# Where squares, low products and norm sums stand at the seams of a two-block network on one core

## What is computed

```python
h = h + 0.5 * rmsnorm_2(swiglu(rmsnorm_2(h, norm_g[0]), ffn1_gu, ffn1_down), norm_g[1])
z = rmsnorm_2(h, norm_g[2]) @ w_in
...
h = h + rmsnorm_2(mixed, norm_g[3])
h = h + 0.5 * rmsnorm_2(swiglu(rmsnorm_2(h, norm_g[4]), ffn2_gu, ffn2_down), norm_g[5])
gate = jax.nn.sigmoid(rmsnorm_2(h, norm_g[6]) @ ple_gate)
h = h + rmsnorm_2((p_i @ ple_proj) * gate, norm_g[7])
```

## Time and profile before

| | |
|---|---|
| median of 3 runs | 2710.93 us (2706.16 to 2711.71) |
| the profiled execution | 2705.2 us, span 2703.4 us |
| PE busy | 2596.4 us, 96% of the span |
| POOL, DVE, ACT busy | 1296.2, 1120.9, 997.9 us |
| mean granted TensorE clock | 0.986 of full speed |
| read from HBM | 230.00 MB, 86 GB/s |

### The profile page before, as it was taken

How to read it: one execution, slowest core, us unless ns; L and a number is a source line. 1 busy time by engine, 2 the same in 40 slices (tenths; PEclk the granted TensorE clock), 3 DMA queues, 4 the chain that set the end, 5 groups by cost and what they waited for, 6 DMA issues and landing times.

```text
span 2703.4 us, 33421 instructions
## 1 busy us (share of the span) xinstructions
PE 2596.4 (96%) x12324; PEld 2080.8 (77%) x12324; DVE 1120.9 (41%) x1680; ACT 997.9 (37%) x1482; POOL 1296.2 (48%) x1664
## 2 busy tenths in 40 slices
PE   6999999999999999899999999999999989999997
PEld 3688777777888877677888877888877767888885
DVE  5588666535221058625221046222028645222025
ACT  5323423524233244444232245222234455232234
POOL 1233467555555444345555454555544344555543
PEclk8999999999999999999999999999999989999998
DMA  6212211132333322112333332333322202333332
GB/s 270 71 55 72 79 45 40 60 115 84 101 98 94 97 92 70 32 63 86 95 101 94 94 94 86 94 97 98 98 88 78 63 24 86 94 96 99 96 96 74
DMA packets 63814, 234.23 MB, mean 87 GB/s; under 512 B 7360, under 2 KB 8000, under 8 KB 63168
## 3 DMA queue, kind: packets, MB, share of 16 engines
q1 hardware_dynamic: 61056, 222.33, 26.2%
q10 hardware_dynamic: 2624, 10.00, 1.0%
HBM read 230.00 MB, written 2.10 MB: 86 GB/s over the span
## 4 chain that ended last, share of the span: by engine, by line
PE 84%; DVE 9%; issue 3%; ACT 2%; POOL 1%; DMA 1%; SPq 0%; DVEq 0%; POOLq 0%; ACTq 0%
PE banks L1881 21%; PE banks L1871 21%; PE banks L1872 21%; PE banks L2221 2%; PE banks L2227 2%; PE banks L2222 2%; DVE tmp L1146 2%; DVE sq_sum L1125 1%; DVE xlo L1153 1%; PE banks L1941 1%; PE banks L2342 1%; DVE h L1149 1%; PE banks L2291 1%; PE banks L2293 1%; PE banks L2292 1%
## 5 line engine op out<-in xcount | busy, mean ns | idle before, releaser
L435 POOL TENSOR_TENSOR wlo<-raw,whi 128x256 fp32r<-128x256 f32 x1584 | 1183.2, 780 | 1262.0 <-ACT whi L538 1261.9
L1871 PE MATMUL banks<-xhi,whi 128*128 128x512 f32 x1920 | 752.5, 392 | 2.3 <-DVE z L1779 2.3
L1872 PE MATMUL banks<-xhi,wlo 128*128 128x512 f32 x1920 | 747.5, 389 | 0.0
L1881 PE MATMUL banks<-xlo,whi 128*128 128x512 f32 x1952 | 735.4, 393 | 10.4 <-DVE xlo L1153 10.3
L538 ACT ACTIVATE whi<-raw 128x1024 fp32r<-128x1024 f32 x396 | 415.1, 1053 | 347.0 <-PE banks L1881 336.6
L1881 PEld LDWEIGHTS banks<-xlo,whi 128*128 128x128 f32 x1952 | 365.2, 188 | 96.7 <-DVE xlo L1153 18.5
L1871 PEld LDWEIGHTS banks<-xhi,whi 128*128 128x128 f32 x1920 | 360.4, 188 | 81.9 <-DVE z L1779 3.1
L1872 PEld LDWEIGHTS banks<-xhi,wlo 128*128 128x128 f32 x1920 | 360.5, 188 | 76.2 <-issue 1.9
L1125 DVE TENSOR_TENSOR sq_sum<-sq_sum,tmp 128x512 f32<-128x512 f32 x110 | 85.2, 774 | 464.6 <-ACT tmp L558 464.6
L1871 PE MATMUL banks<-act_hi,whi 128*128 128x512 f32 x704 | 273.9, 389 | 0.0
L1872 PE MATMUL banks<-act_hi,wlo 128*128 128x512 f32 x704 | 273.9, 389 | 0.0
(11 more groups left out here) (419 smaller groups left out, 3181.3 us busy)
## 6 DMA issues: line engine op xcount, KB each, us to landing
raw<-in_stream SPq DMA_DIRECT2D x396, 512.0 KB, 3.5
ada_raw<-in_stream SPq DMA_DIRECT2D x24, 512.0 KB, 7.3
h<-in_x ACTq DMA_DIRECT2D x2, 2048.0 KB, 12.2
out<-h SPq DMA_DIRECT2D x4, 512.0 KB, 2.6
ctx_raw<-in_ctx ACTq DMA_DIRECT2D x1, 1024.0 KB, 19.6
dft_t<-in_dft_t ACTq DMA_DIRECT2D x1, 1024.0 KB, 5.0
ple_raw<-in_ple ACTq DMA_DIRECT2D x2, 512.0 KB, 3.4
mixpar<-in_mixpar ACTq DMA_DIRECT2D x2, 384.0 KB, 4.2
```

The costliest lines, as they stand in the source:

```text
L435: piece = pool.tensor_tensor(wlo[:, i, s], raw[:, i, s], whi[:, i, s].bitcast(F32), ALU.subtract)
L1871: pe.matmul(acc[acc_of[t]][:], whi[:, u % SLOTS, i], x_h, start=(k == 0), stop=False, skip_group_check=split)
L1872: pe.matmul(acc[acc_of[t]][:], wlo[:, u % SLOTS, i], x_h, start=False, stop=False, skip_group_check=split)
L1881: mm = pe.matmul(acc[acc_of[t]][:], whi[:, u % SLOTS, i], x_l, start=False, stop=(k == k_tiles - 1), skip_group_check=leading and m < leads)
```

## The change

- **Squares later.** ACT squares the stream's tile k - 3 after `xhi` of tile k (`LAG` is 4), and the last three after the loop; DVE adds tile k - 4's squares after `xlo` of k - 1, and the last ones after the loop. The cast of the third unit moves from k = 2 to k = 3.
- **Low products one behind.** `leading` makes the high products of k, then the low ones of k - 1.
- **The stream's sum later.** `pre_sum` stands at the start of output tile 5 in gu and gate, and at (4, 2), before the third k of output tile 4, in in2.
- **The output norm's early sum amid the last tile.** `first_squares` (formerly the first half of `sum_squares`) stands in down, out2 and out1 before the last two k of the last output tile; `last_squares` follows the product as before. After proj both still follow the product. In the first block DVE adds squares m - 1 before it waits for product m.

```diff
 LEADS = 4
 OUT1_LEADS = 2
+LAG = 4
...
                 high_parts(units_to(q) + SLOTS - 1)
                 for k in range(KT):
-                    if k == 2:
+                    if k == 3:
                         high_parts(units_to(q) + SLOTS)
                     if k == 5:
                         high_parts(units_to(q) + SLOTS + 1)
...
+                    if k >= LAG - 1:
+                        squares("h_sq", q, k - LAG + 1, h[:, k - LAG + 1])
+                for k in range(KT - LAG + 1, KT):
                     squares("h_sq", q, k, h[:, k])
...
                             .then_inc(*done("x_low", (q_pre, k - 1)))
-                        sq_add("h_sq", q_pre, k - 1)
+                        if k >= LAG:
+                            sq_add("h_sq", q_pre, k - LAG)
+                for k in range(KT + 1 - LAG, KT) if q_pre != "last" else []:
+                    sq_add("h_sq", q_pre, k)
...
                     t = first_tile["out1"] + m
+                    if m:
+                        sq_add("res_sq", "first", m - 1)
                     v.wait_ge(*after("product", ("out1", m)))
...
-                    if m:
-                        sq_add("res_sq", "first", m - 1)
...
+            def leading(stage, key):
+
+                for k in range(KT):
+                    leading_high(stage, key, k)
+                    if k:
+                        leading_low(stage, key, k - 1)
+                leading_low(stage, key, KT - 1)
...
+            def pre_sum(q):
+
+                pe.wait_ge(*after("sq_added", ("h_sq", q, KT - 1)))
+                pe.matmul(norm_bank[:], ones, sq_sum[:], start=True, stop=True).then_inc(*done("summed", ("pre", q)))
+
+            def first_squares(name, q):
+
+                pe.wait_ge(*after("sq_added", (name, q, KT - 2)))
+                for e, s in enumerate([slice(0, HALF), slice(HALF, SEQ)]):
+                    pe.matmul(bank[4 + e][:, 0:HALF], ones, sq_sum[:, s], start=True, stop=False, skip_group_check=True)
...
                     for k in range(MIX_T):
+                        if (m, k) == (KT - 1, MIX_T - 2):
+                            first_squares("res_sq", "first")
...
                     if s in (0, 2):
-                        product(("gu", layer, s // 2), 2 * FT, KT, xhi, xlo, "x", tile, pre_sum, True)
-                        product(("down", layer, s // 2), KT, FT, act_hi, act_lo, "act", tile)
+                        gu, down = ("gu", layer, s // 2), ("down", layer, s // 2)
+                        leading(gu, tile)
+                        product(gu, 2 * FT, KT, xhi, xlo, "x", tile, LEADS, None, sum_of_stream((LEADS + 1, 0)))
+                        product(down, KT, FT, act_hi, act_lo, "act", tile, 0, None, sum_of_output(FT))
```

More of the change, by code:

```diff
@@ L1861, in product @@
+            def product(stage, tiles, k_tiles, hi, lo, source, key, first=0, after_tile=None, amid=None):
+                for m in range(first, tiles):
+                    t = first_tile[stage] + m
+                    for k in range(k_tiles):
+                        if amid:
+                            amid(m, k)
                         if k == 0 and earlier[t] is not None:
                             pe.wait_ge(*(bank_free(earlier[t]) or (ev.sem("product"), 1)))
-                        u, i = place(stage, m, k, k_tiles, leads)
+                        u, i = place(stage, m, k, k_tiles, first)
@@ L1869, in product @@
                             pe.wait_ge(*after(source + "_high", key(k)))
[L1870 to L1877 removed]
+                        pe.matmul(acc[acc_of[t]][:], whi[:, u % SLOTS, i], hi[:, k], start=(k == 0), stop=False)
+                        pe.matmul(acc[acc_of[t]][:], wlo[:, u % SLOTS, i], hi[:, k], start=False, stop=False)
                         if m == 0:
                             pe.wait_ge(*after(source + "_low", key(k)))
[L1881 to L1882 removed]
+                        mm = pe.matmul(acc[acc_of[t]][:], whi[:, u % SLOTS, i], lo[:, k], start=False, stop=(k == k_tiles - 1))
                         keys = [("unit", u)] if i == UNIT - 1 else []
@@ L2172, in first_block_pe @@
                 rest_of_out()
-                sum_squares("first", "res_sq", "first")
+                last_squares("first", "res_sq", "first")
             def rest_of_out():
```

99 lines of the change are left out of this document (43 added, 56 removed).

## The result

| | before | changed |
|---|---|---|
| median of four runs | 2710.16 us (2706.16 to 2711.71) | 2748.18 us (2742.27 to 2749.56) |
| profiled execution, span | 2705.2, 2703.4 us | 2742.27, 2740.5 us |
| PE busy | 2596.4 us | 2613.5 us |
| mean granted clock | 0.986 | 0.980 |

The ratio is 1.0141, 95% interval 1.0129 to 1.0154: 1.4% slower. Forecast was 2739, range 2718 to 2750. The profiled execution is the fastest of the four, and before's profiled execution (2705.2) is 1 us under the fastest of its four; the 37.1 us between the two spans are the ones accounted for here.

The account below looks back on a forecast made before the run. PE was taken as the bound (84% of the chain), time being gained only where it waits. 2705.2 + 23 for the waits and sums + 7.7 for the clock gave 2736, with half the median's 5.7 offset 2739 us; range 2718 to 2750.

Parts of the forecast that it names:

- all of it longer: Rival, chance 0.05: every wait drags the clock down, in in2 also; about 2745 to 2752 us.
- The output norm's early sum: Ends of down and out2: last tile delayed 0.86 us, what follows 0.27 sooner; +3.6 at six seams, -0.25 at the first.
- Tile 4: Seven seams: tile 4 begins 26.7 us behind the first product instead of 26.33, sum still to come; +8.6 us.
- The sum later: Gu and gate: later stream's sum makes PE wait for the seventh to ninth weight units; +2.7, +4.0 and +1.0 us.
- in2's scores: In in2, first HGRN scores wait 1.7 us for the scaled output tile 4, twice; +3.4 us.
- The clock: Behind the waits at tile 4, clock falls at five or six of seven, 1.4 us each; +7.7, bounds 0 and 9.8.
- the faster one: Rival, chance 0.05: fifth unit cast by 19.6 us behind the seam's first product, tile 4 at 23.5; 2702 us.
- Same waits, but the clock holds: Rival, chance 0.2: the forecast waits come at the seams without the clock falling; 2731 us.
- The later waits don't come: Rival, chance 0.12: units 7 to 9 and the HGRN chain arrive in time, so no waits behind tile 4; 2720 us.

Follow-up runs that it names:

- x10: The changed kernel again, unedited, for a second profile: 2746.67 us, ratio 1.0135.
- x3: Changed kernel with DVE's old order in out1 (residual before the addition of squares) except for the last output tile: 2748.06 us, ratio 1.0142.
- x9: Changed kernel with earlier fifth-unit cast, sum before tile 4's fourth k, early sums behind products, out1's old order, in2 as before the change: 2701.83 us, ratio 0.9971.
- x1: Changed kernel with ACT casting the fifth weight unit before the last xhi instead of behind the last square: 2719.78 us, ratio 1.0045.
- x5: Changed kernel with squares directly behind their input tile again and the third unit's cast back at k = 2: 2733.94 us, ratio 1.0098.
- x2: Changed kernel with the output norm's early sum back behind the last tile in down and out2: 2743.09 us, ratio 1.0128.
- x4: Changed kernel with the stream's sum before output tile 4 in gu, gate and in2: 2722.49 us, ratio 1.0056.

## Why the prediction was right, and where its sizes were off

The mechanism, the sign and the rank of the terms held in the first profile; the time is 9 us over the forecast and 1.8 under the range's upper end. It lies 0.2 us over the forecast's own range (2728 to 2748), in the stretch that I had given to the rival "all of it longer" (2745 to 2752) with 0.05. That rival's condition, low clock behind every wait, did not come. The outer range, drawn out to the rivals' times, took the number in. Three of the nine come from the median, which again lies 5.9 us above the profiled execution, of which I had put on half; six come from the terms. The first of these is chance: in x10 the profiled execution lies 2.4 us above its median. By its own parts:

1. *The output norm's early sum*, +3.6 forecast. Measured 0.75 at each of six seams, +4.5. I let the second sum start as soon as its first half square is there; its two halves came 0.22 sooner, but the norm waits for the last half square too, so only 0.12 reached the next stage. At the first seam the sum paid 0.87 and won 0.95: -0.1 where I had -0.25.
2. *Tile 4*, +8.6 forecast for T + 26.7 and the sum still to come. Measured 26.84 to 26.95: (0.6 + 0.87 + 0.1) times seven, 11. The chain is the one worked out, from the last `xlo` (20.2, found 20.2) over square 7 (22.25, found 22.35) to the cast (22.8, found 22.9). PE was up to 0.25 us later than my 26.7 and loses 0.1 in restarting.
3. *The sum later*, +7.7 forecast. Tile 6 in gu: 0.45 forecast, 0.60 measured; tile 8: 1.0 and 0.65; tile 6 in gate: 0.45 and 0.15; tile 7 in gate: 0.5 and 0.96. Sum 5.0 for four gu and 2.2 for two gates, 7.2.
4. *in2's scores*, 1.7 forecast, 1.58 and 1.81 measured by the gap of starts.
5. *The clock*, +7.7 for five or six falls of 1.4. In the first profile it fell at four of seven tiles 4, for 1.6 each: 6.4. In the second it fell at five, three for 1.4 to 1.6 and two for 2.7 and 2.9: 10.1, over my upper bound of 9.8. By the Trainium skill ("TensorE: Matmul & The Clock Gate", section "HAM oscillation — how this bites in real kernels") every one of the bursts would have started cold; the waits in its example are some 3 to 5 us long. Neither profile shows it at all seven. Behind waits over 3.1 us the clock fell each time, as the Trainium skill has it; waits of 2.8 and less lie outside its figures, and behind them the clock held with one exception. Which seams have the long wait changes between executions.
6. *Missed:* the order of DVE's work in out1, which I took for a neutral rearrangement. It has 1.15 us in the wait for POOL, in every run with that order (2.3 us instead of 1.1 to 1.4), and in the profiled run 1.6 at half clock. x3 shows it. I had costed part of an edit at nothing without asking who waits for the square behind DVE's residual.
7. *Not split up:* in2 to out2 of layer 0 took +7.1, of which the parts above explain 5.4 (0.5 + 0.97 for tile 4 and sum, 1.58 for the scores, 0.75 for the early sum, 1.6 for the clock at tile 4). In the attention low clock is 13.7 us instead of 10.2; half of that is 1.7, which would be the rest, an estimate. No run isolates it; but every version run here, x9 with its unchanged in2 too, takes 2.6 us or more extra in this stretch, with 13.7 to 20.5 us of low clock in the attention. Before's own profile, an execution 5 us below its median, has the least of all. In layer 1 the same parts make 4.2 (0.64 + 0.97 + 1.81 + 0.75) for the +3.9, though the attention has less low clock than before (13.7 instead of 17.1), so these don't add up and stay open.

Of the rivals, the faster one rested on a cast before T + 19.6. x1 is that case made by hand: tile 4 at 23.7 to 25.3, and still 0.45% slower. The late sum's waits, which I had halved in that rival, stay whole, and most of the loss is in in2 (+5.9 and +2.9) and the first gu (+3.6). "Same waits, but the clock holds" (2731) didn't come; x5 is near it, with no fall at tile 4, but its waits there are 0.6 and not 3.2, and it took 2734. "The later waits don't come" (2720) is refuted by the waits at tiles 6, 7 and 8 and at the scores.

## What to carry to other kernels

When work is moved off one engine's path, look at what is queued behind it on the engine that issues the next stage's operand: here ACT's cast of a weight unit stood behind the last of four delayed squares, and the two lines that put the cast first were worth 28 of 38 us. A wait and an operation that used to cover each other (the sum and the wait for tile 4) should be moved together or not at all, and a stage whose outputs have a waiting reader (in2's scores) deserves its own order. Differences of a few us between versions are not read from the total, as long as the clock falls at other places in each execution, but from stretches between fixed products, and best from ones too short to hold such a fall (4.26 and 4.38 us in x2).

## What was unexpected of the hardware

The granted clock falls at different places in two executions of the same kernel. At tile 4 it depended on the length of the wait more sharply than I had thought: in four profiles (the changed kernel twice, x2 and x3) it halved behind all 19 waits of 3.1 to 3.3 us and behind one of nine of 2.2 to 2.8, while behind the 2.26 us before the first product it halves at some seams and not at others, before and after. Length alone doesn't settle the shorter waits: of five equal ones in x4 (1.84 us idle) two fell. What decides there is not shown. The places are coupled: a long half-clock stretch early in a seam makes PE late for tile 4 and shortens the wait there, and the second stretch did not come (both gates of the first profile). So a removed wait can leave the time as it was (x3), and a version can lose in a stage that it didn't touch (x9, in2). A half-clock stretch of 3.4 us in front of the sum cost 1.4 to 1.6 us in gu and gate, one of 6.8 us 2.7 to 2.9.
